# The third token block of the v units: low and high parts of the samples side by side, joined by a shift product

## The reference

```python
h = modulate(x, norm1_g[l], sh1, sc1)
z = h @ w_in[l]                                   # (tokens, 1024) @ (1024, 1536)
u = gelu(z[..., :512]); v_raw = gelu(z[..., 512:1024]); p = z[..., 1024:]
ya, v = chunk_sgu(u, v_raw, ...)                  # layer norm of v per head, mixing over tokens, times u
yb, new_buf = pool_mix(buf, p, ...)               # windows of 2, 4, 8, 16 over p, then a product per group
mix = concatenate([rmsnorm(ya), rmsnorm(yb)]) @ w_out[l]
```

## Time and profile before

| | us |
|---|---|
| median of 3 runs (lowest, highest) | 1541.11 (1540.72, 1541.85) |
| span of the profiled execution, first to last instruction | 1539.8 |
| own time of the profiled execution beyond its span | not listed; the median stands 1.3 above the span |
| TensorE busy | 1520.4 (99%) |
| VectorE busy | 1189.0 (77%) |
| ScalarE busy | 946.2 (61%) |
| GpSimd busy | 94.9 (6%) |
| data moved | 492.59 MB, mean 320 GB/s |

### The profile page before, as it was taken

One profiled execution on the slowest core, in us unless ns is written; L12 is line 12 of the kernel. 1 busy time (PEld: TensorE's weight loads), 2 busy tenths in 40 slices (PEclk: granted clock), 3 DMA queues, 4 the chain that ended last, 5 costly groups with the idle time before them and its releaser, 6 DMA issues.

```text
span 1539.8 us, 21793 instructions
## 1 busy us (share of the span) xinstructions
PE 1520.4 (99%) x8105; PEld 1294.0 (84%) x8105; DVE 1189.0 (77%) x971; ACT 946.2 (61%) x723; POOL 94.9 (6%) x133
## 2 busy tenths in 40 slices
PE   8999999999999999999999999999999999999997
PEld 6787999999977888888888888888888888888885
DVE  4686454444476869898888888888888888889997
ACT  3454423332344557677777777777777777777774
POOL 3220000000002023000000000000000000001001
PEclk9999999999999999999999999999999999999999
DMA  9997944444447859999999999999999999999993
GB/s 351 387 358 268 374 143 157 137 163 137 163 170 296 269 185 361 354 393 394 375 376 387 381 375 388 374 378 378 393 371 385 376 380 374 377 375 374 401 394 122
DMA packets 235378, 492.59 MB, mean 320 GB/s; under 512 B 10155, under 2 KB 16171, under 8 KB 231226
## 3 DMA queue, kind: packets, MB, share of 16 engines
q1 hardware_dynamic: 227110, 472.82, 83.4%
q0 software_dynamic: 5920, 18.57, 3.2%
q10 hardware_dynamic: 2308, 0.64, 0.2%
HBM read 481.86 MB, written 10.36 MB: 320 GB/s over the span
## 4 chain that ended last, share of the span: by engine, by line
PE 95%; DVE 2%; DMA 2%; ACT 1%; SPq 1%; issue 0%; ACTq 0%; DVEq 0%
PE ps L1784 20%; PE ps L1786 20%; PE ps L1785 20%; PE ps L2200 4%; PE ps L2202 4%; PE ps L2201 4%; PE ps L1812 2%; PE ps L2211 2%; PE ps L2212 2%; PE ps L2210 2%; PE ps L2348 2%; PE ps L2154 1%; PE ps L2155 1%; PE ps L2156 1%; PE ps L1917 1%; PE ps L1829 1%
## 5 line engine op out<-in xcount | busy, mean ns | idle before, releaser
L1138 DVE TENSOR_TENSOR w_lo<-raw,w_hi 128x2048 fp32r<-128x2048 f32 x366 | 835.2, 2291 | 172.4 <-ACT w_hi L762 171.1
L762 ACT ACTIVATE w_hi<-raw 128x2048 fp32r<-128x2048 f32 x366 | 701.6, 1917 | 257.7 <-PE ps L1786 161.1
L1784 PE MATMUL ps<-w_hi,split 128*128 128x512 f32 x1392 | 549.0, 394 | 0.6 <-DVE w_lo L1138 0.5
L1786 PE MATMUL ps<-w_hi,split 128*128 128x512 f32 x1392 | 542.5, 390 | 0.0
L1785 PE MATMUL ps<-w_lo,split 128*128 128x512 f32 x1392 | 541.9, 389 | 0.0
L1784 PEld LDWEIGHTS ps<-w_hi,split 128*128 128x128 f32 x1392 | 261.4, 188 | 58.7 <-DVE w_lo L1138 4.3
L1786 PEld LDWEIGHTS ps<-w_hi,split 128*128 128x128 f32 x1392 | 261.3, 188 | 55.3
L1785 PEld LDWEIGHTS ps<-w_lo,split 128*128 128x128 f32 x1392 | 261.6, 188 | 51.7
L2200 PE MATMUL ps<-split,w_hi 128*128 128x320 f32 x432 | 133.8, 310 | 0.0
L2202 PE MATMUL ps<-split,w_lo 128*128 128x320 f32 x432 | 133.5, 309 | 0.0
L2201 PE MATMUL ps<-split,w_hi 128*128 128x320 f32 x432 | 133.5, 309 | 0.0
(11 more groups left out here) (368 smaller groups left out, 1306.7 us busy)
## 6 DMA issues: line engine op xcount, KB each, us to landing
raw<-in_moe_w SPq DMA_DIRECT2D x336, 1024.0 KB, 7.3
raw<-in_ffn_w SPq DMA_DIRECT2D x42, 1024.0 KB, 5.0
raw<-in_ada_w SPq DMA_DIRECT2D x40, 1024.0 KB, 8.9
raw<-in_w_in SPq DMA_DIRECT2D x12, 1024.0 KB, 9.2
raw<-in_ada_w SPq DMA_DIRECT2D x16, 512.0 KB, 11.2
raw<-in_w_out SPq DMA_DIRECT2D x8, 1024.0 KB, 10.3
item_rows<-plain POOLq DMA_DIRECT2D x12, 512.0 KB, 7.8
plain<-in_x_prompt SPq DMA_DIRECT2D x2, 512.0 KB, 3.7
```

The source lines that it names most:

```text
L762: a.activation(w_hi[:, (s0 + j) % SPL], raw[:, (u0 + j) % RAW], ACT.Copy).then_inc(hi_ready, 1)
L1138: v.tensor_tensor(w_lo[:, (s0 + j) % SPL], raw[:, (u0 + j) % RAW], w_hi[:, (s0 + j) % SPL].bitcast(F32), ALU.subtract).then_inc(lo_ready, 1)
L1784: t_.matmul(out, a_hi, b_hi, start=first_, stop=False)
L1786: return t_.matmul(out, a_lo, b_hi, start=False, stop=last_)
```

## The change

The third block holds only the 64 samples. A new tile `s_pair` has, for each chunk, 64 columns with the samples' low parts and 64 with their high parts, side by side in one stationary matrix. Two products (with the high and the low weights) replace three; rows 64 to 127 of bank 6 then hold hi x (w_hi + w_lo), and rows 0 to 63 lo x (w_hi + w_lo), which has one small term more than before (lo x w_lo). To add the low rows onto the high ones, ScalarE copies the low rows to `s_low` and the whole bank to `v_gelu`, a product with a shift matrix (64 rows that map onto columns 64 to 127) puts the low rows into partitions 64 to 127 of bank 4, VectorE adds, and ScalarE runs the Gelu of the third block by itself. `s_pair` is filled by new copies on ScalarE (`sample_hi`) and subtractions on VectorE (`sample_lo`). The declarations of tiles and semaphores, which take no time, are left out here.

```diff
 # gpsimd
         step(g.tensor_copy(pidx[:], idx_now[:].bitcast(I32)))
+        g.memset(shift[:].bitcast(F32), 0.0).then_inc(c_zero, 1)
         g.memset(pp[:, :, 0:PADP], 0.0)
 # scalar
+        def sample_hi(k0, k1):
+
+            a.activation(s_pair[:, k0:k1, 1], hf[:, k0:k1, NP_TOK:T], ACT.Copy).then_inc(s_hi_in, 1)
+
+        def v_activate(l):
+
+            act.wait_ge(split_used, S_IN[l] + 4)
+            a.activation(s_low[0:NS_TOK], ps[0:NS_TOK, 6, :], ACT.Copy)
+            a.activation(v_gelu[:, 2], ps[:, 6, :], ACT.Copy)
+            a.activation(v_gelu[:, 0:2], ps[:, 4:6, :], ACT.Gelu_apprx_tanh).then_inc(s_low_out, 1)
+            act.wait_ge(s_summed, l + 1)
+            a.activation(v_gelu[:, 2], v_gelu[:, 2], ACT.Gelu_apprx_tanh).then_inc(v_out, 1)
+
         def project_in_first():
 
             s = S_IN[0]
             hi_to(s + 4)
+            act.wait_ge(s_lo_in, 2)
             p_copies(0, s + 3)
             hi_to(s + 5)
 
-            act.wait_ge(split_used, s + 4)
-            a.activation(v_gelu[:], ps[:, 4:4 + NBLK, :], ACT.Gelu_apprx_tanh).then_inc(v_out, 1)
+            v_activate(0)
 ...
             ada_rows(SELF_A[1])
+            sample_hi(0, KD)
             hi_to(s + 3)
+            act.wait_ge(s_lo_in, 3)
             p_copies(1, s + 2)
 ...
-            act.wait_ge(split_used, s + 4)
             act.wait_ge(h_ready, 12)
             act.wait_ge(zero_out, 16 * (EXTRA_MAX + 1))
-            a.activation(v_gelu[:], ps[:, 4:4 + NBLK, :], ACT.Gelu_apprx_tanh).then_inc(v_out, 1)
+            v_activate(1)
             state_copy(1)
 ...
         first_hi(0)
+        sample_hi(0, KB)
 ...
         first_hi(2)
+        sample_hi(KB, KD)
         project_in_first()
 # vector
+        ve.wait_ge(c_zero, 2)
+        v.tensor_scalar(shift[0:NS_TOK, NS_TOK:P], ident[0:NS_TOK, 0:NS_TOK], 1.0, None, ALU.mult).then_inc(shift_ready, 1)
         ve.wait_ge(prep_tr, 1)
-        ve.wait_ge(c_zero, 1)
 ...
+        def sample_lo(k0, k1, n_hi):
+
+            ve.wait_ge(s_hi_in, n_hi)
+            v.tensor_tensor(s_pair[:, k0:k1, 0], hf[:, k0:k1, NP_TOK:T], s_pair[:, k0:k1, 1].bitcast(F32),
+                            ALU.subtract).then_inc(s_lo_in, 1)
 ...
                     lo_pair(2 * half + 1)
+                    sample_lo(half * KB, half * KB + KB, half + 1)
                     lo_to(S_IN[l] + 2)
 ...
         def v_stats(l):
 
+            ve.wait_ge(s_joined, l + 1)
+            v.tensor_tensor(v_gelu[:, 2], ps[:, 4, :], v_gelu[:, 2], ALU.add).then_inc(s_summed, 1)
             ve.wait_ge(v_out, l + 1)
 ...
             ada_add(SELF_A[1])
+            sample_lo(0, KD, 3)
             lo_to(s + 3)
 # tensor
             if c == 1:
-                for b in range(NBLK):
-                    tk = slice(VBLK[b], VBLK[b] + P)
-                    ins = mm3(ps[:, 4 + b, :], h_hi[:, kk, tk], h_lo[:, kk, tk], wh[:, k, :], wl[:, k, :],
-                              kk == 0, kk == KD - 1)
-                return ins
+                if k == 0:
+                    pe.wait_ge(s_lo_in, 3 if l else r + 1)
+                for b in range(2):
+                    tk = slice(b * P, (b + 1) * P)
+                    mm3(ps[:, 4 + b, :], h_hi[:, kk, tk], h_lo[:, kk, tk], wh[:, k, :], wl[:, k, :],
+                        kk == 0, kk == KD - 1)
+                t_.matmul(ps[:, 6, :], s_pair[:, kk].rearrange("p a b -> p (a b)"), wh[:, k, :], start=(kk == 0), stop=False)
+                return t_.matmul(ps[:, 6, :], s_pair[:, kk].rearrange("p a b -> p (a b)"), wl[:, k, :], start=False, stop=(kk == KD - 1))
 ...
+        def join_samples(l):
+
+            if l == 0:
+                pe.wait_ge(shift_ready, 1)
+            pe.wait_ge(s_low_out, l + 1)
+            t_.matmul(ps[:, 4, :], shift[0:NS_TOK, :], s_low[0:NS_TOK, :], start=True, stop=True).then_inc(s_joined, 1)
 ...
             ada(SELF_A[0], 2, 4)
+            join_samples(0)
 
             pe.wait_ge(p_out, 2)
 ...
                     mix_pool(1, 3)
                     ada(SELF_B[1], 2, 4)
+                    join_samples(1)
                     pe.wait_ge(st_cp, 2)
                     pe.wait_ge(yb_done, 2 * H)
```

More of the change, by code:

```diff
@@ L39 @@
 T = NP_TOK + NS_TOK
-VBLK = (0, P, T - P)
 BLK = [P, P, NS_TOK]
@@ L169, in views @@
         return out
-    (h_hi, h_lo, g_hi, g_lo), (xs_hi, xs_lo, gt_hi, gt_lo, gt2_hi, gt2_lo, slot_sel, scale_row, shift_row) = views(
+    (h_hi, h_lo, g_hi, g_lo), (xs_hi, xs_lo, gt_hi, gt_lo, gt2_hi, gt2_lo, slot_sel, scale_row, shift_row, s_low), (_, s_pair) = views(
         "split", F32R,
         [(KD, T), (KD, T), (KB, T), (KB, T)],
-        [(KD, P), (KD, P), (KB, P), (KB, P), (KB, P), (KB, P), (D,), (D,), (D,)])
+        [(KD, P), (KD, P), (KB, P), (KB, P), (KB, P), (KB, P), (D,), (D,), (D,), (HALF,)],
+        [(2 * KD * T,), (KD, 2, NS_TOK)])
     scale_row, shift_row = scale_row.bitcast(F32), shift_row.bitcast(F32)
@@ L190, in write_program @@
     ident = sb("ident", [P, P])
+    shift = sb("shift", [P, P], F32R)
     ones = sb("ones", [P, P])
@@ L323, in write_program @@
     v_out = sem("v_out")
+    shift_ready = sem("shift_ready")
+    s_low_out = sem("s_low_out")
+    s_joined = sem("s_joined")
+    s_summed = sem("s_summed")
+    s_hi_in = sem("s_hi_in")
+    s_lo_in = sem("s_lo_in")
     p_out = sem("p_out")
```

## The result

The changed kernel takes 1546.76 us (median of 5 runs, 1546.46 to 1550.77), beside 1541.85 (1540.72 to 1542.01) for the kernel before on the same chip: 4.9 us slower, ratio 1.0037 [1.0027, 1.0048]. The forecast was 1544.6, in a range of 1542.4 to 1546.8: the sign is right, and the size stands at the range's upper end, which the forecast reaches only with one fall of the clock.

What follows compares the result with a forecast made beforehand. TensorE was taken to bound the kernel, with 95% of the span. Delays of 0.85 us in layer 0 and 2.65 in layer 1 make 3.5 us slower: 1541.1 + 3.5 = 1544.6, range 1542.4 to 1546.8.

Steps and rivals of the forecast that it cites:

- The gross gain and where it is lost: Both mixers: 16 fewer products, 3.7 us; unit 1 keeps 0.3 of 0.92, unit 3 all, layer 1's unit 2 nothing.
- The table load behind the copies: ScalarE, both layers: the 1.28 us Gelu table load comes after the two copies and lies open in the chain.
- rival A: Both layers: table load stays ahead of the copies, gaining nothing in layer 0; 2.8 us slower, 1543.9; chance 0.13.
- D: Both chains: ScalarE stands as long again after the open table load; 2.6 us more, 1547.2; chance 0.03.
- The chain of layer 1: Second layer's u unit waits for copies behind the third Gelu: starts at 497.02 in place of 494.38, 2.65 us later.
- Rival B: Both layers: the join's chain hides; 1.3 us faster, 1539.8, or with all 16 products 2.9 faster, 1538.2; chance 0.04.
- C, "The clock falls": Second layer, TensorE working little between 493.5 and 497: one fall to half clock, 1.7 us lost, 1546.3; chance 0.2.
- the term of layer 0: First layer's join: TensorE waits 1.8 us, pooling products start at 67.43 in place of 66.58, 0.85 us later.

Runs made afterwards that it cites:

- early table: Changed kernel with a one-column Gelu ahead of the last weight unit in both layers, loading the table before the copies: 1542.54 us, 1.0010 to before.
- new order: Layer 1 reordered (low part before windows, pooling copies before Gelus, pooling products after unit 3), atop changed kernel with early load, early join, early state copy: 1538.42 us, 0.9974.
- second set's runs: Changed kernel again with no edit, on another chip, against the kernel before: 1548.11 us, ratio 1.0042.
- before with holes: Kernel before, without the change, ScalarE held up by four chained copies of 512 columns in each layer so TensorE waits: 1551.31 us, ratio 1.0062.
- layer 1 alone: The change in the second layer only, the first layer as in the kernel before: 1546.67 us, ratio 1.0027 to before.
- early join: Changed kernel with the shift product writing free bank 0 and waiting for the first copy alone, not the Gelu: 1543.85 us, ratio 1.0006 to before.

## Why the prediction was right in its sign and short in its size

**Right.** *The gross gain and where it is lost*: a part of unit 1, all of unit 3 and nothing of unit 2 survive. The pass behind unit 1 starts at 46.01, released by ScalarE's high part, 0.40 before 46.41 (forecast 0.3). In layer 0 TensorE stands at the join from 67.50 - 2.09 = 65.41 (forecast 65.3); in layer 1 its wait for the windows grew from 0.58 to 1.57, by the time that unit 2 saved.

*The table load behind the copies*: at 65.04 and 493.95, each behind both copies. The early table shows what it costs: with the loads early the kernel is 1.5 us [0.2, 2.9] slower than before, where rival A, in which they stay early, had 2.8; the experiment puts the load ahead of ScalarE's high part, so that layer 0 gains as well, which A left out. As the kernel stands A is out, and so is D: the Gelu starts 1.30 us after the load in both layers. The Trainium skill's further 1.38 us of drain ("ScalarE: Activation LUTs", What ACT_TABLE_LOAD costs) is in no row of the changed kernel either.

*The chain of layer 1*: +2.73 measured, +2.65 forecast, with the wait ahead of the u unit at 2.38 (forecast 2.3), released by ScalarE's copies behind the third Gelu. The steps agree to 0.1 us: load to Gelu 1.30, third Gelu 0.63 (0.58 forecast), addition 0.69, shift product 0.50.

*Rival B*, in which the chain hides, falls for the kernel as it stands. Even with the table early, the join early and the state copy ahead of the Gelus the time is that of before (0.9999) and not 1.3 us under it; that took the new order beside them.

**Short.** The step that failed is rival **C, "The clock falls"**: it was one fall, at a chance of 0.2 and in layer 1 only, and so no part of the sum. Both mixers of the profile got one, of 1.63 and 1.52 us (1.7 by the forecast's row, so the price was right and the chance and the number were not). The argument against it, that TensorE idles 1.5 us between 442 and 495 us and keeps its clock, was from shorter waits (0.71 at 461.59 and 0.58 at 480.95 are the longest that before's rows show there): the waits here are 2.09 in one piece, and 0.67 and 2.38 with one product between them. The forecast had computed both waits (1.8 and 2.3) and put a risk on the second alone.

The smaller miss is the term of layer 0, +1.32 for 0.85. It hung on the arrival of a transfer: ScalarE's high part started at 62.16, released by DMA, in place of 61.68, and the chain behind it moved by some 0.4 (first copy at 63.99 for 63.60, shift product at 67.50 for 67.09). In another profile it starts at 60.92 (early table): the term follows a transfer's time, and the sum gave it no spread.

What came back was not in the forecast either: 0.86 before layer 1, where before's own wait of 0.71 for a transfer swallowed part of the shift, and 1.10 behind the mixers. There both kernels lose 1.7 us to a fall of the clock (0.87 and 0.96; 0.90 and 0.93 after), but at another place: before's stands over the 48 products at 563.20 and comes on top of a wait of 0.83 for VectorE at 560.64, the changed kernel's stands over the six transposes ahead of that wait, which take 3.45 us for 1.88, and the wait is gone. Windows, and then the timeline, of the kernel after:

```profile
556.00:566.00 10.00, 10.00 (x74) 8.88 (x73) 5.96 (x26) 3.97 (x14) 0.82 (x2) 0.90 0.36 137
566.00:576.00 10.00, 9.32 (x62) 7.85 (x60) 6.44 (x20) 8.65 (x15) 6.19 (x15) 0.93 0.08 32
...
564.28 3.45 PE L2339 MATMUL ps<-x,ident 128*128 128x320 f32 x6
567.56 0.31 PE L2346 MATMUL ps<-upto,ones 128*128 128x32 f32 x2
...
570.03 6.20 PE L2358 MATMUL ps<-hf,plain 128*128 128x128 f32 x48 [0.68 <-DVE hf L1627]
```

The sum was therefore 3.5 = 0.85 + 2.65, and what was measured 5.24 = 4.05 + 3.15 - 1.96. That it came as near as the range's upper end is in part luck: what the sum left out, +3.15 and -1.96, has opposite signs. Over the second set's runs the misses are larger: the rest without the clock is 1.5 ± 0.5 in place of 3.5, and the clock, put at nothing, is 4.6 ± 1.1. What swallows the chains in those runs beyond the 0.86 was not traced.

## What to carry to other kernels

A join that crosses three engines is priced from its longest instruction queue, not from its product: the 0.5 us shift product was the smallest part, and a table load, a Gelu and copies that others wait for stood with it in ScalarE's list. Put what others wait for ahead of what nobody waits for, load the table before the data are there, and let a join wait for its own operand alone; here that turned 4.9 us lost into a time equal to before's, and with a new order beside it, which alone gave nothing that can be told, into 3 to 4 us won. And where a forecast opens a wait of two microseconds in front of an engine that was always busy, as here, put the fall of its clock into the sum with its chance, not among the rivals.

## What the runs showed of the hardware that was not expected

**Which waits lower the clock.** Taking the stretches 62 to 76 and 486 to 512 us of the fourteen profiles (before, after, and the twelve), 28 in all: 19 have no wait of TensorE over 0.99 us, and in all of them the granted clock is 1.00. The other nine have one of 1.72 to 3.71 us, and in six of these the clock falls in it or up to 1.6 us behind it: in both mixers of the changed kernel and of before with holes, and in layer 1 of the changed kernel's second profile and of layer 1 alone. It did not fall behind 1.72 in layer 0, nor behind the 2.39 of the early table and of the early join. The Trainium skill's warning of gaps between bursts that drop the clock ("TensorE: Matmul & The Clock Gate", Why this matters for your kernels) is borne out in six cases of nine. But five of the six falls stand at waits that are, each by itself, shorter than the gaps the page warns of; here the measurement decides.

What tells the three others apart stays open. In layer 1 the three profiles of the full join (0.67 to 0.77 of waiting, a product, 2.38 or 2.39 more) all fell and the two with 2.39 alone did not, but before with holes fell behind 2.24 alone. And a repaired wait need not give the clock back at once: the kernel without the join, with full clock in both mixers, lost 1.1 ± 0.7 us more than before elsewhere. That was not traced to a place.
